# Gathering expert rows in a decoder block: u and v rows in one gather of 8 KB, diagonals on VectorE instead of ScalarE

## What is computed

```python
top_s, pos = lax.top_k(cand, PEER_TOPK)
eid = jnp.take_along_axis(cand_id, pos, axis=-1)
g = jax.nn.softmax(top_s, axis=-1)
def chunk(args):
    hc, ec, gc = args                                  # 128 tokens
    a = jnp.einsum('cd,chkd->chk', hc, u_tab[ec])
    w = gc * jax.nn.gelu(a)
    return jnp.einsum('chk,chkd->cd', w, v_tab[ec])
```

## Time and profile before

| | us |
|---|---|
| median of 3 runs | 1071.28 (1065.12 to 1072.61) |
| span of the profiled execution, first to last instruction | 1067.7 |
| first gather of an expert row | 284.9 |
| TensorE busy | 836.5 (78%) |
| VectorE busy | 666.1 (62%) |
| ScalarE busy | 247.8 (23%) |
| GpSimd busy | 703.8 (66%) |
| moved by DMA | 351.89 MB, 330 GB/s over the span |

### The profile page before, as it was taken

How to read it: one execution, slowest core, us unless ns; L and a number is a source line. 1 busy time by engine, 2 the same in 40 slices (tenths; PEclk the granted TensorE clock), 3 DMA queues, 4 the chain that set the end, 5 groups by cost and what they waited for, 6 DMA issues and landing times.

```text
span 1067.7 us, 10182 instructions
## 1 busy us (share of the span) xinstructions
PE 836.5 (78%) x2752; PEld 447.0 (42%) x2752; DVE 666.1 (62%) x1588; ACT 247.8 (23%) x617; POOL 703.8 (66%) x626
## 2 busy tenths in 40 slices
PE   5897679998937579998878797886677777766778
PEld 4665546657922134443334364552222222222223
DVE  5799975514789996673444548899644444444443
ACT  2452444442221113241102022212111021010120
POOL 2386645520277777777878774776777777777773
PEclk9999889999969989999999999998999999999899
DMA  9965772467689999999999999999899999999997
GB/s 316 355 237 184 264 258 82 160 233 267 241 297 374 343 360 353 370 318 372 400 400 396 398 393 369 377 405 396 274 373 387 379 378 399 369 347 359 356 378 271
DMA packets 121723, 351.89 MB, mean 330 GB/s; under 512 B 10761, under 2 KB 23121, under 8 KB 121681
## 3 DMA queue, kind: packets, MB, share of 16 engines
q0 software_dynamic: 73728, 268.47, 66.7%
q1 hardware_dynamic: 46256, 82.88, 21.7%
q10 hardware_dynamic: 1696, 0.04, 0.1%
HBM read 350.30 MB, written 1.05 MB: 329 GB/s over the span
## 4 chain that ended last, share of the span: by engine, by line
PE 28%; DVE 24%; DMA 24%; issue 12%; POOL 9%; ACT 2%; POOLq 0%; SPq 0%; DVEq 0%
DMA ring<-in_peer_v,idx 15%; PE ps_y L1480 15%; DMA ring<-in_peer_u,idx 7%; DVE wide L563 5%; POOL ring L496 5%; POOL ring L503 4%; DVE ring L877 4%; DVE wide L569 2%; PE bank L1430 2%; PE ps_y L1292 1%; PE bank L1421 1%; PE bank L1393 1%; PE bank L1375 1%; PE ps_y L1293 1%; PE ps_y L1294 1%
## 5 line engine op out<-in xcount | busy, mean ns | idle before, releaser
L1480 PE MATMUL ps_y<-ring,diag 128*128 128x512 f32 x1012 | 493.6, 623 | 170.4 <-DMA ring<-in_peer_v,idx 152.0
L877 DVE CUSTOM_DVE_ANT_0 ring<-ring,gates 128x1024 f32<-128x1024 f32 x240 | 288.9, 1224 | 222.6 <-DMA ring<-in_peer_u,idx 221.8
L1480 PEld LDWEIGHTS ps_y<-ring,diag 128*128 128x128 f32 x1012 | 183.7, 195 | 459.1 <-issue 355.9
L496 POOL DMA_INDIRECT ring<-in_peer_u,idx x256 | 289.6, 1131 | 95.6 <-issue 63.7
L503 POOL DMA_INDIRECT ring<-in_peer_v,idx x256 | 286.8, 1120 | 81.1 <-issue 65.4
L479 POOL TENSOR_TENSOR w_lo<-ring,w_hi 128x512 fp32r<-128x512 f32 x80 | 115.2, 1460 | 86.8 <-ACT w_hi L1006 36.4
L1169 ACT ACTIVATE diag<-ident,ew 128x128 f32<-128x128 f32 x253 | 85.4, 392 | 143.6 <-PE ps_y L1480 139.1
L563 DVE SCALAR_TENSOR_TENSOR wide<-ring,silu,wide 128x512 f32<-128x512 f32 x56 | 66.7, 1192 | 1.6
L489 POOL COPY idx<-eid 128x16 int32 (+1 forms) x16 | 6.4, 402 | 71.1 <-DVE eid L849 71.1
L1292 PE MATMUL bank<-w_hi,hT_hi 128*128 128x512 f32 x96 | 42.2, 439 | 10.4 <-issue 8.4
L1006 ACT ACTIVATE w_hi<-ring 128x512 fp32r<-128x512 f32 x80 | 46.1, 623 | 17.9 <-PE bank L1294 17.8
(11 more groups left out here) (194 smaller groups left out, 875.4 us busy)
## 6 DMA issues: line engine op xcount, KB each, us to landing
ring<-in_w_ada SPq DMA_DIRECT2D x12, 2048.0 KB, 9.0
ring<-in_w_in SPq DMA_DIRECT2D x10, 2048.0 KB, 10.3
ring<-in_w_peer_q SPq DMA_DIRECT2D x4, 2048.0 KB, 8.0
late_ring<-in_w_peer_q SPq DMA_DIRECT2D x8, 1024.0 KB, 17.2
ring<-in_w_out SPq DMA_DIRECT2D x2, 2048.0 KB, 10.9
ring<-in_peer_u,idx POOLq DMA_INDIRECT x256, 6.3
ring<-in_peer_v,idx POOLq DMA_INDIRECT x256, 6.4
late_ring<-in_w_out SPq DMA_DIRECT2D x4, 1024.0 KB, 16.6
```

Source lines behind the costliest of these rows:

```text
L496: pool.indirect_dma_start(u_row(k), None, peer_u[0], bass.IndirectOffsetOnAxis(ap=idx[:, r, k:k + 1], axis=0)).then_inc(s_u[k % NU], 16)
L877: dve.tensor_tensor_reduce(u_row(k), u_row(k), h2[:, t, :], 1.0, 0.0, ALU.mult, ALU.add, adot[:, par, k:k + 1]).then_inc(s_ufree, 1)
L1480: ins = pe.matmul(ps_y[:, cut], diag[:, k % ND, :], v_row(k)[:, cut], start=(first and k == 0), stop=(last and k == TOPK - 1))
```

## The change

- The host lays the two tables side by side into one, `peer_uv`, of 16384 rows of 2048 columns, and one gather of 8 KB a partition fetches a row's u and v parts. Instead of 8 + 8 slots there are 8 of twice the size (`NP`). GpSimd issues 256 gathers, takes the ids straight from `eid`, and all is written out without a device loop. A slot is free once the row's v part is added (`s_added`).
- Gelus are made for a pair of rows. VectorE makes the diagonal itself, from `ident`, the gate and the gelu, as one instruction with two scalars; there is no `ew`. In pair p it makes them behind dot 2p for pair p - 1.
- TensorE does slot p's work and then adds pair p. It no longer waits for the landing of v, since the diagonal implies it.
- The slots: attention 18 to 1, up 35 to 20, out 45 to 29, scores 55 to 39, and the choices as in the diff. `finish(0)` is in slot 64.
- Scratch tiles of the choices (`cand`, `i16f`, `pw`, `pf`) move from tiles that attention uses into `wide`.
- The last group is done like any other: no `last_dots`, `last_rows`, `DVE_ROWS`.

```diff
-SLOT = {"choice": ((None, None, 7, 11, 15), (59, 63, 67, 71)), "attention": 18, "up": 35, "out": 45, "scores": 55}
+SLOT = {"choice": ((None, None, 5, 11, 19), (46, 50, 54, 58)), "attention": 1, "up": 20, "out": 29, "scores": 39}
...
+            for n in range(NG * TOPK):
+                if n < NP:
+                    if n % 2 == 0:
+                        await_chunk_read(pool, chunk_no["peer", n // 2])
+                else:
+                    pool.wait_ge(s_added, n - NP + 1)
+                if n % TOPK == 0:
+                    pool.wait_ge(s_eid, n // TOPK + 1)
                 pool.indirect_dma_start(
+                    uv_row(n), None, peer_uv,
+                    bass.IndirectOffsetOnAxis(ap=eid[:, n:n + 1], axis=0)).then_inc(s_uv[n % NP], 16)
...
+            def dot(n):
+
+                dve.wait_ge(s_uv[n % NP], 16 * (n // NP + 1))
+                at = n % (2 * TOPK)
+                dve.tensor_tensor_reduce(u_row(n), u_row(n), h2[:, n // P, :], 1.0, 0.0,
+                                         ALU.mult, ALU.add, adot[:, at:at + 1]).then_inc(s_dot, 1)
+
+            def diagonals(pair):
+
+                dve.wait_ge(s_gelu, pair + 1)
+                for n in (2 * pair, 2 * pair + 1):
+                    c_ = n % TOPK
+                    if n >= ND:
+                        dve.wait_ge(s_added, n - ND + 1)
+                    dve.tensor_scalar(diag[:, n % ND, :], ident[:], g_sb[:, n:n + 1], gel[:, c_:c_ + 1],
+                                      ALU.mult, ALU.mult).then_inc(s_diag, 1)
...
+            behind.setdefault(HEADS * PAIRS, []).append(lambda: finish(0))
+            for pair in range(NG * PAIRS):
+                dot(2 * pair)
+                if pair:
+                    diagonals(pair - 1)
+                dot(2 * pair + 1)
+                run(pair)
+            diagonals(NG * PAIRS - 1)
             finish(1)
...
+            def gelu(pair):
+
+                first = 2 * pair
+                at, two = first % (2 * TOPK), slice(first % TOPK, first % TOPK + 2)
+                act.wait_ge(s_dot, first + 2)
+                if first >= TOPK:
+                    act.wait_ge(s_diag, first - TOPK + 2)
+                act.activation(gel[:, two], adot[:, at:at + 2], ACT.Gelu_apprx_tanh).then_inc(s_gelu, 1)
...
+            for pair in range(NG * PAIRS):
+                gelu(pair)
+                run(pair)
...
+            def add_rows(pair):
+
+                for n in (2 * pair, 2 * pair + 1):
+                    first, last = n % P == 0, n % P == P - 1
+                    pe.wait_ge(s_diag, n + 1)
                     for h in range(2):
                         cut = slice(h * HALF, (h + 1) * HALF)
+                        ins = pe.matmul(ps_y[:, cut], diag[:, n % ND, :], v_row(n)[:, cut], start=first, stop=last)
+                        if h == 0 and last:
                             ins.then_inc(s_half, 1)
+                    ins.then_inc(s_added, 1)
...
+            for pair in range(NG * PAIRS):
+                for stage in behind.get(pair, ()):
+                    stage()
+                if pair == HEADS * PAIRS:
+                    pe.wait_ge(s_ytaken, 2)
+                add_rows(pair)
```

More of the change, by code:

```diff
@@ L35 @@
 NLO = 4
-NU = 8
-NV = 8
+NP = 8
 ND = 8
-DVE_ROWS = (NV, NV + 2, NV + 4)
 NB = 6
@@ L871, in run @@
                     stage()
-            def dots(i, par, t, slot=None):
-                for k in range(TOPK):
-                    dve.wait_ge(s_u[k % NU], i * (16 * (TOPK // NU)) + 16 * (k // NU + 1))
-                    dve.tensor_tensor_reduce(u_row(k), u_row(k), h2[:, t, :], 1.0, 0.0,
-                                             ALU.mult, ALU.add, adot[:, par, k:k + 1]).then_inc(s_ufree, 1)
-                    if slot is not None and k % 2 == 1 and k < TOPK - 1:
-                        run(slot + k // 2)
-                dve.wait_ge(s_gelu, i + 1)
-                dve.tensor_tensor(ew[:, par, :], g_sb[:, bass.ds(i * TOPK, TOPK)], gel[:],
-                                  ALU.mult).then_inc(s_ew, 1)
-                if slot is not None:
-                    run(slot + PAIRS - 1)
@@ L887, in last_dots @@
-            def last_dots():
-                i, par = NG - 1, (NG - 1) % 2
-                for k in range(TOPK):
-                    dve.wait_ge(s_u[k % NU], i * (16 * (TOPK // NU)) + 16 * (k // NU + 1))
-                    dve.tensor_tensor_reduce(u_row(k), u_row(k), h2[:, 1, :], 1.0, 0.0,
-                                             ALU.mult, ALU.add, adot[:, par, k:k + 1]).then_inc(s_ufree, 1)
-                    if k % 4 == 3:
-                        four = slice(k - 3, k + 1)
-                        dve.wait_ge(s_gelu, i + k // 4 + 1)
-                        dve.tensor_tensor(ew[:, par, four], g_sb[:, i * TOPK + k - 3:i * TOPK + k + 1],
-                                          gel[:, four], ALU.mult).then_inc(s_ew, 1)
@@ L942, in _ @@
                 choose_experts(0, n)
-            for i in range(HEADS + 1):
-                dots(i, i % 2, i // HEADS, PAIRS * i)
-            finish(0)
-            dots(HEADS + 1, 1, 1, PAIRS * (HEADS + 1))
-            with dve.Fori(1, HEADS // 2 - 1) as n:
-                for j in range(2):
-                    dots(n * 2 + (HEADS + j), j, 1)
-            dots(NG - 2, 0, 1)
-            last_dots()
-            last_rows()
+            behind.setdefault(HEADS * PAIRS, []).append(lambda: finish(0))
[6 more added lines that the diff above has]
+            diagonals(NG * PAIRS - 1)
             finish(1)
@@ L1159, in run @@
                     stage()
-            def gelu(i, par):
-                act.wait_ge(s_ufree, NU + (i + 1) * TOPK)
-                if not isinstance(i, int) or i:
-                    act.wait_ge(s_ew, i)
-                act.activation(gel[:], adot[:, par, :], ACT.Gelu_apprx_tanh).then_inc(s_gelu, 1)
-            def diagonal(i, par, k):
-                act.wait_ge(s_vfree, i * TOPK + (k + 1 - ND + NV))
-                act.activation(diag[:, k % ND, :], ident[:], ACT.Copy,
-                               scale=ew[:, par, k:k + 1]).then_inc(s_diag, 1)
-            def diagonals(i, par, slot=None):
-                act.wait_ge(s_ew, i + 1)
-                for k in range(TOPK):
-                    diagonal(i, par, k)
-                    if slot is not None and k % 2 == 1:
-                        run(slot + k // 2 - 1)
+            def gelu(pair):
[5 more added lines that the diff above has]
+                act.activation(gel[:, two], adot[:, at:at + 2], ACT.Gelu_apprx_tanh).then_inc(s_gelu, 1)
             attention(0, 0)
```

139 lines of the change are left out of this document (23 added, 116 removed).

## The result

| | before | after |
|---|---|---|
| median of 4 runs each | 1068.88 (1065.12 to 1072.61) | 1121.24 (1119.41 to 1125.00) |
| span of the profiled execution | 1067.7 | 1120.8 |
| busy: TensorE, VectorE, ScalarE, GpSimd | 836.5, 666.1, 247.8, 703.8 | 863.3, 723.3, 214.4, 409.1 |

The ratio is 1.048, with an interval of 1.043 to 1.052: the changed kernel is slower by 52 us. The forecast was slower by 13.

A forecast was written before the change was run, and what follows sets the result against it. GpSimd's issue of 512 gathers was taken to bound the expert stage (730 of 773 us). After: 457 + 543 + 37 + 25 + 8 + 11 = 1081 us of span, 13 more than before, so 1084 us; range 1045 to 1122.

The forecast's parts named there:

- The turn: Attention slots: VectorE and TensorE take turns, 8.2 us a slot for the first head group, about 7.5 for the second.
- VectorE's wait ahead of the scores: Sign that the forecast is right: VectorE idle 3 to 4 us ahead of each score add in slots 1 to 14.
- The start: Start of the expert stage: GpSimd waits for query weights before row 6; TensorE reads those until 302 us, adding only after.
- the walk to row 38: Slots 1 to 16 summed by turns, second steps and choices: slot free for row 38 at about 451 us, landed at 457.
- From row 38 on: Rest of the expert stage: gathers run back to back, 217 rows at 2.50 us, 543 us.
- the estimate from two kinds of packets: DMA: a line of 8 ns fixed plus 0.0402 ns a byte makes 8 KB packets 2.3% cheaper, 2.50 us a row.
- Late weights 37, choices 25, 8 for the rest: After row 38: 14 weight loads 37 us, second-tile choices in slots 46 to 61 25, group 4's choice and longer-held slots 8.
- The tail: From the last landing to the end: dot, gelu, diagonals, weight load, adds and the finish, 11 us.
- GpSimd at 2.55 us a gather: Rival, 0.09: GpSimd's gather price doubles with the bytes and it stays the bound, 1095 to 1105 us.
- Eight whole slots too few: Rival, 0.14: slots held longer make rows 2.5 to 2.9 us; at 2.7, 43 us more, 1127; decides above 10 us landing.
- The turns cost nothing: Rival, 0.14: TensorE's adds early enough that VectorE never waits in slots 0 to 16; row 38 near 412, 1039 us.

The follow-up runs named there:

- the second filling: The changed kernel with products that add zero put on TensorE ahead of the adds in slots 0 to 14 (8 excepted): 1105.63 us.
- scores before adds: The changed kernel with TensorE doing slot p's work ahead of the adds of pair p-1 instead of behind them: 1071.69 us.
- the choices split: The changed kernel with pair p-1 added behind slot p's work, each choice in three parts, and the second tile's choices four slots earlier: 1049.09 us.

## Why the prediction was wrong in size

The direction, the mechanism and the place were right, and 1121 lies just inside the range (1045 to 1122); the size was not: 13 us forecast, 52 measured. By its own terms:

- *The turn, "dot 1.15, diagonal 0.25, the semaphore and weight load 0.3, eight matmuls 3.7 ...: 8.2 us a slot".* This is the step that failed: the term for the eight matmuls. 3.7 us came from the one row at 414.35, in a slot in which TensorE hadn't paused. The same sum gave TensorE a pause of dot, diagonals and handover in each turn, and I didn't ask what pauses do to the eight matmuls behind them. The kernel before had the answer once, in an attention slot behind a choice, where TensorE idled 5.78 us and then added for 6.08 (and again 4.57 us at 428.54):

```profile
397.65 0.66 PE L1384 MATMUL bank<-ident,score 128*128 128x128 f32 x2 [5.78 <-DVE score L731]
398.10 6.08 PE L1480 MATMUL ps_y<-ring,diag 128*128 128x512 f32 x8
```

  Eleven groups of adds ahead of row 38 took 5.17 to 6.72 us, 65.2 us instead of 40.7: 24.5 us of the 28 by which row 38 was late (the expectation of the second filling leaves one of them out). Where the clock was up the turn was 8.03 us, so the other parts of the sum were right (the second diagonal starts 0.26 us behind the first, each 0.34 long). Of the signs named, VectorE's wait ahead of the scores was there, but as 5.3 to 6.7 us in slots 1 to 3 and not 3 to 4. And 40 gathers were issued by 481 us, not 55.
- *The start.* The first adds began at 307.80, where I had 302. TensorE ended the queries at 305.2 (the stage began 2.7 us later in this execution, which differs from one to the next), and the first gelu stood behind ScalarE's copies of these and a table load until 307.16; VectorE waited 5.3 us for it (the row of L851 above has 15.0 us <-ACT gel in all). These 5.8 us and the 24.5 make 30.3 for the 28.2 measured, so the rest of the walk to row 38 came out 2 us shorter than I had it.
- *From row 38 on, "217 rows x 2.50".* Two slots late in the stage, four rows, take 9.9 to 10.0 us together, 2.485 us a row: right, and with it the estimate from two kinds of packets. After:

```profile
q0 software_dynamic: 36864, 268.45, 59.8%
```

  59.8% of 16 engines' 1120.8 us is 290.9 ns a packet of 7282 B in the mean, against the 2 x 154.5 = 309 ns before, 6% less, more than the 2.3% of the line (in the earlier trace rows a share of 1.04 goes with 398 GB/s and one of 1.02 with 407, so GB/s is the better witness). The Trainium skill's rule of about 358 GB/s ("DMA: Bandwidth & Descriptors", section Bandwidth) doesn't bind here, as 421 shows. The same skill says elsewhere ("HBM Reference", section Specifications (TRN2)) that a core alone streams at about 425, and that about 358 is the share of each with both cores streaming; this kernel runs on one core, and the 421 agree.
- *Late weights 37, choices 25, 8 for the rest.* From the issue of row 38 to the end there were 641.6 us, where the forecast had 1081 - 451 = 630. 3 us less for the rows and a tail of 10.7 instead of 11 leave 15 us that the middle cost over the 70 given. Part of it may be the second choices: with these split and laid earlier, 382 GB/s instead of 340 are moved from 660 to 800 us. How much of the 15 us that is wasn't measured.
- *The tail, 11 us.* The last dot starts at 1110.10, the end is at 1120.8: right.
- *GpSimd at 2.55 us a gather.* Refuted: with the 0.30 us between two it is 1.125 + 0.30 = 1.43 us, for twice the bytes.
- *Eight whole slots too few.* Refuted as the bound of the late stage, although the sign that I named came: landing took 11.1 us in the median, over the 10 from which I let it decide. DMA share 1.01 and 421 GB/s in that stretch show that it didn't. That its 1127 lies near the measured 1121 is chance.
- *The turns cost nothing, row 38 near 412, 1039.* With scores before adds it came at 427.9 and 1071.7. So the order gave away the 49 us, but with the other order the change still brings no gain where the kernel before takes about 1070: what it moves more from 850 to 1000 us (421 GB/s instead of 367) it gives up from 285 to 481 (299 instead of 340) and from 660 to 800 (340 instead of 361). The gain of 1 to 3% came with the choices split, 421.9 and 1049. Whether the kernel before would gain by the split as well is open.

## What to carry to other kernels

When a change makes two engines wait for each other, don't sum the turn with the durations of a busy stretch alone. Look in the trace for the same instructions behind a pause, and put both into the range: on TensorE here the same matmuls cost 3.7 us or up to 6.7. Before one engine's work is made to depend on another's of the same step, put whatever doesn't depend on it first in its order: adding a pair behind the next slot's work instead of ahead of it was worth 49 us here. Work on VectorE that must be done while transfers run is worth cutting into pieces shorter than the issued transfers last; the runs here support that, with the slots moved at the same time.

## What the runs showed of the hardware

- In turns of 11 to 13 us in which TensorE paused for 2.1 to 3.1 us, its granted clock was at half for 3.4 to 6.8 us at a time, but the length of a pause didn't settle it: behind 2.13 us the same adds took 6.72 us once and 3.70 the next time. Filling the pauses with useless products brought the time at half clock from 78 to 20 us between 300 and 480, and the whole kernel was 16 us faster.
- A gather of 128 rows costs GpSimd 0.94 us alone, for 4 KB and for 8 KB rows. When it starts during a dot product it ends 0.8 us behind the dot (1.56 us long at 952.07 before, 1.57 at 480.93 after, 1.01 where only 0.2 us of the dot were left); when it has started before one it isn't stretched, and neither is the dot.
- Two gathers of 4 KB a row moved 404 GB/s and one of 8 KB 421, with a DMA share of 1.02 and 1.01.
- The kernel before took 3 to 4% longer on two of the chips than on the others, while versions with 8 KB rows kept their time (1049.1 and 1050.3 us for the same kernel on one chip of either kind). Why wasn't found.
